# The router of the expert layer: its logits computed by quarters of x inside the output projection, its norm, scale and shift applied as factors where rows are read

## What is computed

```
x = x + g1 * (mixer(...) @ w_out)
h = rmsnorm(x, norm2_g) * (1.0 + sc2) + sh2          # sc2, sh2: 2048 numbers each
glog = h @ rg_w + rg_b                               # 4 groups
elog = h @ re_w + re_b                               # 32 experts
gsel = argmax(glog); top 2 of the 8 experts of that group; gates from two softmaxes
x = x + g2 * sum over the 2 experts of gate * (silu(h @ w_gate[e]) * (h @ w_up[e])) @ w_down[e]
```

## Time and profile before

| | |
|---|---|
| time, median of 3 runs | 2673.03 us (2672.11 to 2675.17) |
| the profiled execution's own time, and its span | 2675.53 us, 2673.7 us |
| PE busy | 2438.7 us (91%) |
| DVE, ACT, POOL busy | 884.1, 720.5, 914.4 us |
| HBM read | 714.03 MB |
| weight loads of the experts | 402 MB (192 loads of 2 MB) |

### The profile page before, as it was taken

One profiled execution on the slowest core, in us unless ns is written; L12 is line 12 of the kernel. 1 busy time (PEld: TensorE's weight loads), 2 busy tenths in 40 slices (PEclk: granted clock), 3 DMA queues, 4 the chain that ended last, 5 costly groups with the idle time before them and its releaser, 6 DMA issues.

```text
span 2673.7 us, 29788 instructions
## 1 busy us (share of the span) xinstructions
PE 2438.7 (91%) x12149; PEld 1578.2 (59%) x12149; DVE 884.1 (33%) x1393; ACT 720.5 (27%) x1143; POOL 914.4 (34%) x408
## 2 busy tenths in 40 slices
PE   7999889998997998997989698799999999999997
PEld 5666567875665676776877576544444444444443
DVE  4122444111234346388453643212111111111113
ACT  4333344443343443433222343101100000110000
POOL 5455454864553559774434246000000000000000
PEclk9999999999998999998999789799999999999999
DMA  8666546576663654342222228399999999999994
GB/s 326 244 252 252 221 189 252 205 302 235 248 241 152 248 236 148 126 157 93 72 91 95 95 88 328 137 393 427 428 429 429 428 428 429 428 429 428 429 428 199
DMA packets 63227, 719.59 MB, mean 269 GB/s; under 512 B 14848, under 2 KB 15232, under 8 KB 19104
## 3 DMA queue, kind: packets, MB, share of 16 engines
q1 hardware_dynamic: 56512, 713.94, 65.6%
q10 hardware_dynamic: 6032, 2.87, 0.4%
q0 software_dynamic: 592, 1.49, 0.2%
HBM read 714.03 MB, written 4.24 MB: 269 GB/s over the span
## 4 chain that ended last, share of the span: by engine, by line
PE 44%; issue 37%; DVE 11%; ACT 3%; DMA 2%; POOL 2%; ACTq 0%; DVEq 0%; POOLq 0%; SPq 0%
PE bank L1794 15%; PE bank L1805 7%; PE bank L335 6%; PE bank L1843 3%; PE bank L345 3%; PE bank L1762 2%; DVE qk_t L840 2%; DMA weight_ring<-in_w_in_dram 2%; ACT w_hi_parts L2020 1%; POOL weight_ring_parts L1719 1%; PE bank L1878 1%; PE bank L1895 1%; DVE qk_t L838 1%; DMA weight_ring<-in_w_out_dram 1%; PE bank L425 1%
## 5 line engine op out<-in xcount | busy, mean ns | idle before, releaser
L1719 POOL TENSOR_TENSOR weight_ring_parts<-weight_ring,w_hi_parts 128x1024 fp32r<-128x1024 f32 (+2 forms) x368 | 872.3, 2386 | 705.2 <-ACT w_hi_parts L2020 704.7
L2020 ACT ACTIVATE w_hi_parts<-weight_ring 128x1024 fp32r<-128x1024 f32 (+2 forms) x368 | 379.1, 1042 | 693.0 <-PE bank L1805 305.1
L1114 POOL TENSOR_TENSOR rms_out<-rms_in,minus_half 128x2 f32<-128x2 f32 x2 | 3.4, 1682 | 984.0 <-DVE rms_in L1439 971.3
L1794 PE MATMUL bank<-w_hi_parts,h_t_parts 128*128 128x512 f32 (+1 forms) x768 | 221.0, 413 | 6.3 <-ACT w_hi_parts L2020 6.3
L1219 PE MATMUL bank<-weight_ring,qk_t 128*64 128x512 f32 x1024 | 224.1, 592 | 0.0
L1794 PE MATMUL bank<-w_hi_parts,x_res_parts 128*128 128x512 f32 (+1 forms) x768 | 204.4, 391 | 0.0
L1805 PE MATMUL bank<-weight_ring_parts,h_t_parts 128*128 128x512 f32 (+1 forms) x768 | 196.5, 385 | 0.0
L1794 PEld LDWEIGHTS bank<-w_hi_parts,h_t_parts 128*128 128x128 f32 x768 | 139.5, 198 | 55.2 <-issue 21.7
L1794 PEld LDWEIGHTS bank<-w_hi_parts,x_res_parts 128*128 128x128 f32 x768 | 145.7, 196 | 31.2
L1219 PEld LDWEIGHTS bank<-weight_ring,qk_t 128*64 128x64 f32 x1024 | 77.7, 137 | 142.7 <-issue 142.7
L1805 PEld LDWEIGHTS bank<-weight_ring_parts,h_t_parts 128*128 128x128 f32 x768 | 142.8, 192 | 29.6
(11 more groups left out here) (424 smaller groups left out, 3426.8 us busy)
## 6 DMA issues: line engine op xcount, KB each, us to landing
...
```

The lines of the kernel that those rows point to most:

```text
L1719: nc.gpsimd.tensor_tensor(weights(split, True), weights(split, False), rounded(split).bitcast(f32), ALU.subtract)\
L1794: nc.tensor.matmul(bank[2 * (v % 2) + t][:, 0:width], part(k, t), w[:, n, :], start=first and part is hi and n == 0, stop=False)
L2020: A_(rounded(split), weights(split, False), ACT.Copy).then_inc(w_hi_ready, 1)
```

## The change

The router's weights W are scaled once, by rows, with (1+sc2)·g, and sh2 is folded into the bias, so that the logits are r·(x @ W') + b'. PE can then transpose and multiply the quarters of x as they come, one unit later each, inside the output projection (`x_chunk` ahead of piece 2, `route` ahead of piece 5), and only the last quarter is left behind it. ACT sums the squares by quarters. h is no longer formed: ACT writes Y = x·r, the gather takes rows of Y, and scale and shift are applied where ACT copies the gathered (and thereby transposed) rows out, 128 columns at a time, as a factor and an addend for each partition. Six small loads (shift and scale as columns, the router's weights and biases) move from SP's queue, where they stood in the output projection, to ACT's, in the input projection; two loads of whole rows are dropped.

```diff
+    def x_chunk(n):
+        pe.wait_ge(m.xo, 4 * LAYERS + 2 + n)
+        for j in (2 * n, 2 * n + 1):
+            transposes(j % 2 == 0, [X[:, t, (2 * j + b) * P:(2 * j + b + 1) * P] for b in (0, 1) for t in range(TT)])
...
+    def route(n):
+        copied()
+        if n == 0:
+            pe.wait_ge(m.rw_ready, 1)
+            pe.wait_ge(m.rb_ready, 1)
+        for k in range(4 * n, 4 * n + 4):
+            for t in range(TT):
+                i = 2 * (k % 2) + t
+                last = mm(bank[4 + t][:, 0:36], (m.hs if k % 4 > 1 else m.hid)[:, i * P:(i + 1) * P], m.rw[:, k, :], start=k == 0, stop=k == KB - 1)
+        return last
...
-        unit(v, m.y_hi, m.y_lo, {} if n else {i: [lambda j=i + 3: y_columns(j)] for i in range(1, 5)})
+        steps = {2: [lambda n=n: x_chunk(n - 1)], 5: [lambda n=n: route(n - 1)]} if n else {i: [lambda j=i + 3: y_columns(j)] for i in range(1, 5)}
+        if n == 1:
+            steps[1] = [shift_sum]
+        unit(v, m.y_hi, m.y_lo, steps)
+    x_chunk(3)
+    route(3).then_inc(m.rt_ready, 1)
...
+    act.wait_ge(m.h_split, 8)
+    act.wait_ge(m.mod_out, 16 * 24)
+    for dst, at in ((m.shc, 3 * D), (m.gsc, 4 * D)):
+        act.dma_start(dst[:, :], m.mod[0, at:at + D].rearrange("(k p) -> p k", p=P), allow_slow_non_contiguous=True).then_inc(m.router_in, 16)
+    a = m.a
+    act.dma_start(m.rw[:, :, 0:4], a["router_group_w_2"][0].rearrange("(k p) n -> p k n", p=P)).then_inc(m.router_in, 16)
+    act.dma_start(m.rw[:, :, 4:36], a["router_expert_w_2"][0].rearrange("(k p) n -> p k n", p=P)).then_inc(m.router_in, 16)
+    act.dma_start(m.rb[:, 0:4], a["router_group_b_2"].partition_broadcast(P)).then_inc(m.router_in, 16)
+    act.dma_start(m.rb[:, 4:36], a["router_expert_b_2"].partition_broadcast(P)).then_inc(m.router_in, 16)
...
+    def squares(n):
+        act.wait_ge(m.xo, 4 * LAYERS + 2 + n)
+        if n:
+            act.wait_ge(m.x2_squared, n)
+        for t in range(TT):
+            last = A_(m.junk3[t], X[:, t, n * U:(n + 1) * U], ACT.Square, accum_out=m.ssx[:, 0, t, n:n + 1])
+        last.then_inc(m.x2_squared, 1)
+    for n in range(3):
+        to(UNITS2 + n + 1, 2)
+        squares(n)
+        copy(m.hid, bank[6][:, :])
     split_to(PIECES_ALL - 1)
+    squares(3)
+    copy(m.hid, bank[6][:, :])
...
+    dve.wait_ge(m.router_in, 16 * 6)
+    cols = lambda x: x[:, :].unsqueeze(2).to_broadcast([P, KB, EXPERTS + GROUPS])
+    V.tensor_tensor(m.rw_sh, m.rw[:, :, :], cols(m.shc), ALU.mult)
+    link(V.scalar_tensor_tensor(m.gsc[:, :], m.gsc[:, :], 1.0, m.small_all[:, LAYERS * SMALL + KB:], ALU.add, ALU.mult))
+    V.tensor_reduce(m.rw_sum, m.rw_sh.rearrange("p k n -> p n k"), AX.X, ALU.add).then_inc(m.rb_part, 1)
+    V.tensor_tensor(m.rw[:, :, :], m.rw[:, :, :], cols(m.gsc), ALU.mult).then_inc(m.rw_ready, 1)
...
+    dve.wait_ge(m.x2_squared, 4)
+    link(V.tensor_reduce(m.rin[:, 0:2], m.ssx[:, 0, :, :], AX.X, ALU.add))
+    V.tensor_scalar(m.rin[:, 0:2], m.rin[:, 0:2], 1.0 / D, EPS, ALU.mult, ALU.add).then_inc(m.rin_ready, 1)
+    copy(m.hs, bank[7][:, :])
...
-    def route(j):
-        for k in (2 * j, 2 * j + 1):
-            for t in range(TT):
-                last = mm(bank[t][:, 0:36], m.HT[:, k, t * P:(t + 1) * P], m.rw[:, k, :], start=k == 0, stop=k == KB - 1)
-        return last
-    for j in range(8):
-        if j % 2 == 0:
-            pe.wait_ge(m.h2_ready, 1 + j // 2)
-        t, ready, cop, ps = (ta, m.ta_ready, m.ta_copied, bank[6]) if j % 2 == 0 else (td, m.td_ready, m.td_copied, bank[7])
-        pe.wait_ge(cop, t.now())
-        for i, (b, tt) in enumerate([(b, tt) for b in (0, 1) for tt in range(TT)]):
-            last = nc.tensor.transpose(ps[:, i * P:(i + 1) * P], H[:, tt, (2 * j + b) * P:(2 * j + b + 1) * P], m.ident)
-        last.then_inc(ready, 1)
-        t.next()
-        if j == 2:
-            pe.wait_ge(m.rows2_in, 16 * 8)
-        if j >= 2:
-            route(j - 2)
-    pe.wait_ge(m.ta_copied, ta.now())
-    pe.wait_ge(m.td_copied, td.now())
-    route(6)
-    route(7).then_inc(m.rt_ready, 1)
...
-    act.wait_ge(m.xo, 4 * LAYERS + 1 + 4)
+    act.wait_ge(m.rms_ready, LAYERS * PER["rout"] + 5)
     for t in range(TT):
-        last = A_(m.junk2[t], X[:, t, :], ACT.Square, accum_out=m.ss[:, t:t + 1])
-    last.then_inc(m.sq_ready, 1)
-    for i, j in enumerate(range(0, 8, 2)):
-        act.wait_ge(m.ta_ready, LAYERS * PER["ta"] + TA2 + i + 1)
-        A_(m.HT[:, 2 * j:2 * j + 2, :], bank[6][:, :], ACT.Copy).then_inc(m.ta_copied, 1)
+        last = A_(Y[:, t, :], X[:, t, :], ACT.Copy, scale=m.rms[:, t:t + 1])
+    last.then_inc(m.h2_ready, 1)
...
-            A_(m.xg[:, 4 * q:4 * q + 4, :], bank[2 + (tx.n - 1) % 2][:, :], ACT.Copy).then_inc(m.tx_copied, 1)
+            for i in range(4):
+                k = 4 * q + i
+                last = A_(m.xg[:, k, :], bank[2 + (tx.n - 1) % 2][:, i * P:(i + 1) * P], ACT.Identity,
+                          scale=m.gsc[:, k:k + 1], bias=m.shc[:, k:k + 1])
+            last.then_inc(m.tx_copied, 1)
...
-    dve.wait_ge(m.sq_ready, sq + 1)
-    V.tensor_scalar(m.rin[:, 0:2], m.ss[:, 0:2], 1.0 / D, EPS, ALU.mult, ALU.add).then_inc(m.rin_ready, 1)
-    dve.wait_ge(m.rows2_in, 16 * 8)
-    link(V.scalar_tensor_tensor(m.sc2, m.sc2, 1.0, m.gn2, ALU.add, ALU.mult))
-    dve.wait_ge(m.rms_ready, rr + 1)
-    for q in range(4):
-        c = slice(q * U, (q + 1) * U)
-        for t in range(TT):
-            last = V.scalar_tensor_tensor(Y[:, t, c], X[:, t, c], m.rms[:, t:t + 1], m.sc2[:, c], ALU.mult, ALU.mult)
-        link(last)
-        V.tensor_tensor(Y[:, :, c], Y[:, :, c], m.sh2[:, c].unsqueeze(1).to_broadcast([P, TT, U]), ALU.add).then_inc(m.h2_ready, 1)
-    for i, j in enumerate(range(1, 8, 2)):
-        dve.wait_ge(m.td_ready, LAYERS * PER["tdr"] + TD2 + i + 1)
-        V.tensor_copy(m.HT[:, 2 * j:2 * j + 2, :], bank[7][:, :]).then_inc(m.td_copied, 1)
...
-        last = V.tensor_tensor(lg[:, t, :], bank[t][:, 0:36], m.rb, ALU.add)
+        last = V.scalar_tensor_tensor(lg[:, t, :], bank[4 + t][:, 0:36], m.rms[:, t:t + 1], m.rb[:, :], ALU.mult, ALU.add)
```

More of the change, by code:

```diff
@@ L293, in second_tensor @@
 def second_tensor(nc, m, pe):
-    PROJ, HT, QK, Y, bank, ident = m.PROJ, m.HT, m.QK, m.Y, m.bank, m.ident
+    PROJ, HT, QK, X, Y, bank, ident = m.PROJ, m.HT, m.QK, m.X, m.Y, m.bank, m.ident
     mm = nc.tensor.matmul
@@ L547, in y_columns, with shift_sum @@
         turn(j, [rows[t][:, b * P:(b + 1) * P] for b in (0, 1) for t in range(TT)])
+    def shift_sum():
+        copied()
+        pe.wait_ge(m.rb_part, 1)
+        mm(bank[5][:, 64:100], m.ones, m.rw_sum, start=True, stop=True).then_inc(m.rb_sum, 1)
+    def x_chunk(n):
[3 more added lines that the diff above has]
+    def route(n):
+        copied()
+        if n == 0:
[6 more added lines that the diff above has]
+        return last
     for j in range(4):
@@ L983, in second_vector @@
         dve.wait_ge(m.xo, 4 * LAYERS + 2 + n)
+        if n == 0:
+            dve.wait_ge(m.rb_sum, 1)
+            V.tensor_tensor(m.rb[:, :], m.rb[:, :], bank[5][:, 64:100], ALU.add).then_inc(m.rb_ready, 1)
+        if n < 3:
+            copy(m.hs, bank[7][:, :])
+    dve.wait_ge(m.x2_squared, 4)
+    link(V.tensor_reduce(m.rin[:, 0:2], m.ssx[:, 0, :, :], AX.X, ALU.add))
+    V.tensor_scalar(m.rin[:, 0:2], m.rin[:, 0:2], 1.0 / D, EPS, ALU.mult, ALU.add).then_inc(m.rin_ready, 1)
+    copy(m.hs, bank[7][:, :])
     return steps
@@ L1045, in moe_buffers @@
     m.sca, m.scb = pb[:, 2 * S:3 * S], pb[:, 3 * S:4 * S]
-    m.g2, m.fng = m.sh2, m.slots[0][:, 0:D]
+    m.fng = m.slots[0][:, 0:D]
     rq = m.ropeq[:, :, :, :].rearrange("p t h n -> p (t h n)")
@@ L1063, in moe_sync @@
     sp.wait_ge(m.on_done, TT)
-    for dst, src in ((m.gn2, a["norm2_g_2"]), (m.sh2, m.mod[:, 3 * D:4 * D]),
-                     (m.rb[:, 0:4], a["router_group_b_2"]), (m.rb[:, 4:36], a["router_expert_b_2"])):
-        sp.dma_start(dst, src.partition_broadcast(P)).then_inc(m.rows2_in, 16)
-    sp.dma_start(m.rw[:, :, 0:4], a["router_group_w_2"][0].rearrange("(k p) n -> p k n", p=P)).then_inc(m.rows2_in, 16)
-    sp.dma_start(m.rw[:, :, 4:36], a["router_expert_w_2"][0].rearrange("(k p) n -> p k n", p=P)).then_inc(m.rows2_in, 16)
     sp.dma_start(m.cst3, a["cst3"]).then_inc(m.rows2_in, 16)
+    sp.dma_start(m.g2, m.mod[:, 5 * D:6 * D].partition_broadcast(P)).then_inc(m.g2_in, 16)
     def pair_loads(p):
@@ L1163, in moe_tensor @@
     pe.wait_ge(m.zeroed, 1)
+    pe.wait_ge(m.h2_ready, 1)
     def gather(tx, gm):
@@ L1271, in moe_scalar @@
     A_(m.v[3], m.v[3], ACT.Exp).then_inc(m.rexp_ready, 1)
+    act.wait_ge(m.rw_ready, 1)
     act.wait_ge(m.rounds_ready, 1)
@@ L1557, in program @@
     m.gsc, m.shc = sb("scale_cols", [P, KB]), sb("shift_cols", [P, KB])
+    m.rw, m.rb = sb("router_w", [P, KB, EXPERTS + GROUPS]), sb("router_b", [P, EXPERTS + GROUPS])
+    m.router_in, m.rw_ready, m.rb_part, m.rb_sum, m.rb_ready, m.x2_squared = (
```

(8 more changed lines are left out.)

22 lines of the change are left out of this document (9 added, 13 removed).

## The result

| | before | after |
|---|---|---|
| median of 4 runs, side by side | 2674.10 us (2672.11 to 2678.56) | 2705.77 us (2701.19 to 2710.77) |
| profiled execution, span | 2673.7 us | 2701.9 us |
| its own time | 2675.53 us | 2703.75 us |

A forecast was written before the change was run, and what follows sets the result against it. PE was taken to set the pace in the output projection, and PE's own chain in the loop. Terms -28.7 + 7.8 + 15.5 + 0.8 + 12.5 = +7.9 us on 2673.03 gave 2681 us, range 2668 to 2692.

The forecast's parts named there:

- The stretch behind the projection: From the output projection's last matmul to the logits: 36.9 us shrink to 8.2 (7.5 to 8.7), a gain of 28.7.
- The root: Behind the projection: POOL takes 2.67 us for the root, which is there 7.5 us after the last matmul.
- the gather ahead of the loop: Gather before the experts' loop: only its last group's copies lose time, 0.8 us.
- PE work moved into the projection: Output projection: added transposes, small matmuls and the shift's product cost PE 7.8 us (7.5 to 8.1).
- None should wait: x's quarter is ready 2.8 behind a unit: Output projection: PE's moved transposes stand behind 4.6 us of matmuls, so they wait for nothing.
- Copies of the gathered rows: Experts' loop: four copies take 1.44 us, each of 16 pairs grows by 1.08; 15.5 in all after load waits.
- my choice between two bounds: Gathered rows' copies: operands read one after the other, 1.08 us a pair, or together, 0.51 (rival, chance 0.17).
- the rivals: Loads cheap 0.12, operands together 0.17, both 0.07, loads hold ACT 27 us 0.08; also the stretch not shortened, given little.
- Six small loads on ACT: Input projection: load issues hold ACT, and PE behind it, for 12.5 us, all of it counted.
- its lower bound of 7.5: Input projection: ACT is held only 7.5 us if the small loads get going ahead of the bulk load.

The follow-up runs named there:

- experiment 1: The changed kernel with one plain ACT copy of 512 columns per group of gathered rows, scale and shift left out: 2668.77 us, 0.9984 of the kernel before.
- experiment 6: The changed kernel with the transposes of x's quarter ahead of piece 4 instead of 2, router's products ahead of piece 6 instead of 5: 2708.71 us.
- experiment 9: The changed kernel with four copies of 128 columns that have the factor from memory but no addend: 2691.22 us, 1.0063 of the kernel before.
- experiment 4: The changed kernel with twelve useless PE transposes in each pair, where PE otherwise waits 1.35 us for the last group's copies: 2686.44 us.

## Why the prediction was wrong, step by step

*The stretch behind the projection, -28.7.* Right: -28.2 with the gather included, for which -27.9 was predicted. The root took POOL 0.70 and not 2.67, which changed nothing, since PE's last products were the later of the two: they ended 9.0 us behind the last matmul (1680.37 + 1.90 against 1673.3), where 8.2 was predicted and 8.7 was the upper end. That the whole still fits within 0.3 us is luck in part: behind the logits about 1 us less was lost than I had counted, 0.6 of it at the gather ahead of the loop (47.2 against the 47.0 of experiment 1's one copy, so 0.2 and not 0.8).

*PE work moved into the projection, 7.8.* Right within a microsecond: 100.3 - 91.5 = 8.8 in experiment 6, where nothing waits. The mark at the y transposes isn't steady, since PE's clock is not the same there in every execution (at this place 0.50 in 1556 to 1564 before, 1.00 in 1564 to 1568 and 0.59 in 1568 to 1572 in the changed kernel). From the rounding at 1573.89 to the end of the last matmul it is 79.8 us in the kernel before, 92.4 in all eight kernels with the change's order and 88.2 in all four with experiment 6's: 8.4 for the work, 4.2 for the waits.

*"None should wait: x's quarter is ready 2.8 behind a unit".* Wrong. The 2.8 was read behind the last unit, where POOL is idle. Within the projection DVE's two products took 4.60 in the kernel before too; the row was there, and I had taken the one of another moment. It cost 3.0 us, or 4.2 by the steadier mark. The Trainium skill, "SBUF — State Buffer", section "Who interferes with whom", says that a DVE instruction with two inputs in SBUF contends with a GpSimd instruction that reads SBUF, over ports that one of them holds exclusively, while one with at most one input there (outside some faster modes) does not. By that rule, the trace agrees: the products with x and p_buf take 4.6 instead of 1.4 beside a busy POOL, the ones ahead of them, with a bank and one tile in SBUF, 1.29 in both places.

*Copies of the gathered rows, 1.08 a pair.* The length was right: 1.44 predicted for four, 1.50 measured, and pairs with an undisturbed clock grew by 59.7 - 58.5 = 1.2. That both operands cost was my choice between two bounds, and experiment 9 bears it out. The Trainium skill, "ScalarE: Activation LUTs", section "What ACT_TABLE_LOAD costs", gave 93 ns for each operand; the runs show 0.35 for four, 88 ns. Only the estimate of 1.64 from its formula was above the 1.50.

*What the sum left out: PE's clock.* This is the step that failed most. I had written that PE waits longer for the last group (0.47 in the earlier trace rows, 1.35 measured), and costed that wait at its own length. In fact PE's clock fell behind it and its neighbour in most pairs, and each fall cost 1.7 us: 17 to 19 us in all (experiment 4), as much as the copies themselves. The stretch behind the projection stood in the prediction at the lower clock level; that a wait in the loop might lead there too was not among the rivals. The Trainium skill, "TensorE: Matmul & The Clock Gate", section "A second HAM failure mode: psum-queue depth-cycling", tells of another kernel, in which short idle times of PE between groups of matmuls made its clock swing between the two levels. The trace shows such a swing too, here with only two idle times close together once in each pair of some 60 us (1.35 and 0.76 to 0.96), and it would have been a rival.

*Six small loads on ACT, 12.5.* Mechanism right, the hold too long: ACT stood for 9.7, and 8.2 us were lost at that place. The cost was near the 12.5 all the same, 10.8 in the changed trace and 11.1 on average (6 to 11 by the medians), but in part by luck: 2.8 of it came through PE's clock near 1375, which the prediction didn't have. The first four issues went otherwise than written: 0.39, 1.04, 2.73 and 5.75, not 0.4, 6.6, 2 and 2. The wait did not sit on the second column load but on the router's two, since the small loads got going ahead of the bulk load: that is the condition that the prediction gave for its lower bound of 7.5, and it came true for the first two of the four.

The terms as the traces have them: -28.2 for the stretch, 8.8 and 3.0 in the projection, 7.8 up to it (8.2 for the loads, 3.8 by which the execution was ahead, and 3.4 lost between, 2.8 of them by PE's clock near 1375), 16 x 1.16 = 18.6 for the copies and 11 x 1.7 = 18.7 for the clock (ten pairs between the silus and the last one): 28.7 us, against 28.2 between the spans.
